# Dense expert values with tokens as output rows, an end that runs tile by tile, and a new split of the low parts between VectorE and GpSimd

## What is computed

```python
h = rmsnorm(x, g_mix)
q, k, v, f, B, C, xc, g_attn, g_conv = split(h @ w_in)
a = forgetting_attention(q, k, v, log_sigmoid(f + b_f))      # 8 heads x 64
c = B * causal_depthwise_conv3(C * xc)
x = x + (sigmoid(g_attn) * (a @ W_up_attn) + sigmoid(g_conv) * (c @ W_up_conv)) @ w_out
h = rmsnorm(x, g_ffn)                                        # expert retrieval ("PEER")
ids, gates = top 16 of 128 x 128 product keys, for each of 8 heads
x = x + sum over the 128 chosen of gates * gelu(h . u[id]) * v[id]
x = x + sigmoid(rmsnorm(x, g_ple) @ w_ple_gate) * (p @ w_ple_proj)
return rmsnorm(x, g_final)
```

## Time and profile before

| | |
|---|---|
| median of 3 runs | 1931.49 us (1930.06 to 1932.35) |
| the profiled execution | 1934.96 us |
| its span, first to last instruction | 1933.1 us |
| PE busy | 1854.1 us (96%) |
| DVE busy | 1271.2 us (66%) |
| POOL busy | 1137.2 us (59%) |
| ACT busy | 750.4 us (39%) |
| mean granted clock of TensorE | 0.983 |

### The profile page before, as it was taken

How to read it: one execution, slowest core, us unless ns; L and a number is a source line. 1 busy time by engine, 2 the same in 40 slices (tenths; PEclk the granted TensorE clock), 3 DMA queues, 4 the chain that set the end, 5 groups by cost and what they waited for, 6 DMA issues and landing times.

```text
span 1933.1 us, 24399 instructions
## 1 busy us (share of the span) xinstructions
PE 1854.1 (96%) x9045; PEld 1611.0 (83%) x9045; DVE 1271.2 (66%) x2244; ACT 750.4 (39%) x1190; POOL 1137.2 (59%) x666
## 2 busy tenths in 40 slices
PE   6999999989999999999999999989999998989987
PEld 5777788878888888888888888889999998989976
DVE  6355422357899778888988960146688677768643
ACT  5433322333232344444444442433344443434331
POOL 6322344433354476776767764478888888877430
PEclk9999999989999999999999999999999999999998
DMA  5222122322344435454554546659999999999511
GB/s 196 78 66 66 58 99 95 120 67 87 103 140 145 147 131 215 172 180 174 186 192 173 185 172 235 216 166 323 331 328 343 325 347 326 327 335 349 194 33 44
DMA packets 187509, 360.90 MB, mean 187 GB/s; under 512 B 17408, under 2 KB 123904, under 8 KB 185728
## 3 DMA queue, kind: packets, MB, share of 16 engines
q1 hardware_dynamic: 143328, 231.77, 36.5%
q0 software_dynamic: 22528, 67.19, 9.4%
q10 hardware_dynamic: 21536, 60.40, 8.4%
HBM read 298.44 MB, written 60.82 MB: 186 GB/s over the span
## 4 chain that ended last, share of the span: by engine, by line
PE 75%; POOL 17%; issue 3%; DMA 2%; DVE 1%; ACT 1%; ACTq 0%; SPq 0%; DVEq 0%
PE bank L745 36%; PE bank L553 11%; PE bank L555 10%; PE bank L554 10%; POOL wl L492 7%; POOL picked L520 6%; PE bank L770 2%; POOL gout L527 2%; POOL rows_h L527 2%; POOL rows_ex L527 1%; DMA raw<-stream 1%; PE bank L649 1%; PE bank L669 1%; PE bank L723 1%; PE bank L639 0%
## 5 line engine op out<-in xcount | busy, mean ns | idle before, releaser
L492 POOL TENSOR_TENSOR wl<-raw,wh 128x1024 fp32r<-128x1024 f32 x298 | 737.9, 2478 | 670.3 <-ACT wh L847 668.7
L847 ACT ACTIVATE wh<-raw 128x1024 fp32r<-128x1024 f32 x338 | 356.5, 1055 | 383.7 <-PE bank L555 195.2
L553 PE MATMUL bank<-hh,wh 128*128 128x512 f32 (+1 forms) x1056 | 396.6, 376 | 30.5 <-DVE x L1400 19.2
L745 PE MATMUL bank<-hh,wh 128*128 128x512 f32 x1024 | 400.3, 391 | 0.8 <-ACT scores L1002 0.8
L745 PE MATMUL bank<-hh,wl 128*128 128x512 f32 x1024 | 400.9, 391 | 0.0
L745 PE MATMUL bank<-hl,wh 128*128 128x512 f32 x1024 | 399.6, 390 | 0.0
L555 PE MATMUL bank<-hh,wl 128*128 128x512 f32 (+1 forms) x1056 | 389.4, 369 | 0.0
L554 PE MATMUL bank<-hl,wh 128*128 128x512 f32 (+1 forms) x1056 | 389.3, 369 | 0.0
L553 PEld LDWEIGHTS bank<-hh,wh 128*128 128x128 f32 x1056 | 202.6, 192 | 60.7 <-DVE x L1400 21.5
L745 PEld LDWEIGHTS bank<-hh,wl 128*128 128x128 f32 x1024 | 192.2, 188 | 37.8
L745 PEld LDWEIGHTS bank<-hl,wh 128*128 128x128 f32 x1024 | 192.3, 188 | 36.9
(11 more groups left out here) (211 smaller groups left out, 2503.6 us busy)
## 6 DMA issues: line engine op xcount, KB each, us to landing
raw<-stream SPq DMA_DIRECT2D x338, 512.0 KB
score_dram<-gout ACTq DMA_DIRECT2D x128, 256.0 KB, 2.5
gate_dram<-stage ACTq DMA_DIRECT2D x12, 2048.0 KB, 7.5
gate<-gate_dram SPq DMA_DIRECT2D x16, 1536.0 KB
score_in<-score_dram SPq DMA_DIRECT2D x128, 192.0 KB
x<-xT SPq DMA_DIRECT2D x4, 512.0 KB, 5.5
picked<-score_dram,score_at POOLq DMA_INDIRECT x128
outT<-outb SPq DMA_DIRECT2D x8, 256.0 KB, 2.2
```

Source lines behind the costliest of these rows:

```text
L492: nc.gpsimd.tensor_tensor(wl[:, n % SL, :], raw[:, n % RAW, :], wh[:, n % SL, :].bitcast(F32), ALU.subtract).then_inc(lo_done, 1)
L553: nc.tensor.matmul(out, ah, bh, start=start, stop=False)
L745: last = nc.tensor.matmul(psum[u % 2][:], w(weights, U_DENSE + u, c), tokens[c][:, :], start=c == 0 and which == 0, stop=c == DC - 1 and w ...
L847: nc.scalar.activation(wh[:, n % SL, :], raw[:, n % RAW, :], ACT.Copy).then_inc(hi_done, 1)
```

## The change

The V units keep the layout in which they lie in DRAM: one unit is one block of 128 experts by 1024 features, loaded in pieces of 4 KB. The activations become the stationary operand and the values the moving one: per block 3 token tiles x 2 halves x 3 = 18 matmuls of 512 columns, summed over all 128 blocks in three pairs of PSUM banks. `x` itself is transposed into these banks first, by float32 matmuls with the identity (`turn_x`, 8 for each tile), so `add_values` goes. `act_h` and `act_l` are one ring of 8 blocks, and the GELU uses two banks instead of three. The sum over the fetched rows is kept in SBUF (`sparse_sum`), starts from `x` of tile 0, and has 8 row slots and a lag of 5 steps instead of 6 and 4. DVE makes the low part of every second V unit. The end has tokens as rows and runs tile by tile in the order 1, 2, 0, 3: the squares are summed inside ACT's instruction, the norm is applied by a matmul with a scaled identity which also transposes (`turn_scaled`), and the last four blocks are computed tile by tile.

```diff
-HB = 4
+LAST = 4
+RING = 8
-ROWS = 6
-ROW_LAG = 4
+ROWS = 8
+ROW_LAG = 5
+END_ORDER = (1, 2, 0, 3)
 def low_by_dve(n):
-    return U_V0 + SL <= n < U_PLE and n % 3 == 0
+    return U_V0 + SL <= n < U_PLE and n % 2 == 0
...
+def turn_x(tile, pair):
+    for c in range(DC):
+        last = nc.tensor.matmul(pairs[pair][:, c * P:(c + 1) * P], x[:, c, tile * P:(tile + 1) * P], ident[:],
+                                start=c % 4 == 0, stop=tile == 0 and c % 4 == 3)
+    return last
...
+                if u == NK - TAIL_U + 1:
+                    pe.wait_ge(quad_out, QUADS)
+                    turn_x(0, 2).then_inc(x_turned, 1)
+                    turn_x(1, 1)
+                elif u == NK - TAIL_U + 5:
+                    pe.wait_ge(sum_copied, 1)
+                    turn_x(2, 2)
+def block_values(b, tile):
+    at = slice((tile - 1) * P, tile * P)
+    for half in range(2):
+        cols = slice(half * T, (half + 1) * T)
+        last = three(pairs[tile][:, cols], act_h[:, b % RING, at], act_l[:, b % RING, at],
+                     wh[:, (U_V0 + b) % SL, cols], wl[:, (U_V0 + b) % SL, cols], False, b == NK - 1)
+    return last
+for b in range(NK - LAST):
+    wait_low(pe, U_V0 + b)
+    pe.wait_ge(wsplit, b + 1)
+    for tile in range(1, TT):
+        if b == 0 and tile == TT - 1:
+            pe.wait_ge(wsplit, RING)
+            turn_x(tile, tile)
+        last = block_values(b, tile)
+    last.then_inc(unit_used, 1)
+def turn_scaled(tile, pair):
+    for c in range(DC):
+        last = nc.tensor.matmul(pairs[pair][:, c * P:(c + 1) * P], xt[tile][:, c * P:(c + 1) * P], scaled[:, tile, :],
+                                start=True, stop=True)
+    return last
+for tile in range(1, TT):
+    for b in range(NK - LAST, NK):
+        ...
+        last = block_values(b, tile)
+    if tile > 1:
+        pe.wait_ge(x_copied, tile - 1)
+        turn2(tile - 2)
+pe.wait_ge(row_added, HK)
+turn2(2)
...
 def add_row(k):
     dve.wait_ge(rows_in[k % ROWS], 16 * (k // ROWS + 1))
-    nc.vector.scalar_tensor_tensor(out=picked_sum[:], in0=vrow[k % ROWS], scalar=weight, in1=picked_sum[:],
-                                   op0=ALU.mult, op1=ALU.add).then_inc(row_added, 1)
+    nc.vector.scalar_tensor_tensor(out=sparse_sum[:], in0=rows[:, k % ROWS, :], scalar=pick_w[:, k:k + 1],
+                                   in1=sparse_sum[:], op0=ALU.mult, op1=ALU.add).then_inc(row_added, 1)
...
+def std_of(tile):
+    nc.scalar.activation(squares[:], xt[tile], ACT.Square, accum_out=ssq2[:, tile:tile + 1]).then_inc(squared2, 1)
+    act.wait_ge(squared2, tile + 1)
+    nc.scalar.activation(std2[:, tile:tile + 1], ssq2[:, tile:tile + 1], ACT.Sqrt, bias=eps[:],
+                         scale=1.0 / D).then_inc(std2_ready, 1)
+std_of(0)
+for n in range(U_PLE - SL, U_PLE - LAST):
+    next_high(n)
+std_of(1)
+std_of(2)
+high2(0)
+std_of(3)
+for n in range(U_PLE - LAST, U_PLE):
+    next_high(n)
+high2(1)
+high2(2)
+embeddings(0)
+high2(3)
+embeddings(1)
...
+for half in range(2):
+    for i in range(TT):
+        ple_gate(half, i)
+        if half == 1 and i == 2:
+            turn3(0)
+            turn3(1)
+turn3(2)
+turn3(3)
```

More of the change, by code:

```diff
@@ L65 @@
 TAIL_U = 18
-GELU_BANKS = 3
-OUT_BANKS = 3
+LAST = 4
+RING = 8
 TILE_ORDER = (1, 2, 3, 0)
@@ L165, in peer_block_kernel @@
         x = sb("x", [P, DC, T], F32)
[L166 to L174, removed]
+        tokens = ExitStack()
+        hh = sb("hh", [P, DC, T], F32R, tokens)
+        hl = sb("hl", [P, DC, T], F32R, tokens)
+        tokens.close()
+        rows = sb("rows", [P, ROWS, D], F32)
         raw = sb("raw", [P, RAW, UW], F32)
@@ new lines, in _, with weights, embedding @@
+            pe.wait_ge(row_added, HK)
+            turn2(2)
+            def weights(part, n, parts, k, order):
+                return part[:, n % SL, :].rearrange(order, j=4, k=parts)[:, k]
+            def embedding(half, tile):
+                i = TT * half + tile
+                if i >= 2:
+                    pe.wait_ge(emb_out, i - 1)
+                bank = psum[4 + i % 2].rearrange("p (j w) -> p j w", j=4)
+                for k in range(2):
+                    at = slice(k * T + tile * P, k * T + (tile + 1) * P)
+                    n = U_PLE + 1 + half
+                    last = three(bank, wh[:, U_PLE % SL, at], wl[:, U_PLE % SL, at],
+                                 weights(wh, n, 2, k, "p (j k w) -> p k j w"), weights(wl, n, 2, k, "p (j k w) -> p k j w"),
+                                 k == 0, k == 1)
+                last.then_inc(emb_ready, 1)
@@ new lines, in _, with ple_gate @@
+            pe.wait_ge(x_copied, 2)
+            for half in range(2):
+                wait_low(pe, U_PLE + 1 + half)
+                for tile in range(TT):
+                    embedding(half, tile)
+                if half == 0:
+                    pe.wait_ge(x_copied, 3)
+                    turn2(3)
+            def ple_gate(half, i):
+                tile, step = END_ORDER[i], TT * half + i
+                cols = slice(tile * P, (tile + 1) * P)
+                if half == 0:
+                    pe.wait_ge(hl2_ready, 2 * (i + 1))
+                if step >= 2:
+                    pe.wait_ge(sg_ready, step - 1)
+                bank = psum[6 + step % 2].rearrange("p (j w) -> p j w", j=4)
+                for c in range(DC):
+                    n = U_GATE + 4 * half + c // 2
+                    if i == 0 and c % 2 == 0:
+                        wait_low(pe, n)
+                    last = three(bank, hh[:, c, cols], hl[:, c, cols],
+                                 weights(wh, n, 2, c % 2, "p (j k w) -> p k j w"), weights(wl, n, 2, c % 2, "p (j k w) -> p k j w"),
+                                 c == 0, c == DC - 1)
+                last.then_inc(gate_ready, 1)
@@ L838, in _, with turn3 @@
+            def turn3(i):
+                pe.wait_ge(diag3_ready, i + 1)
+                if i >= 2:
+                    pe.wait_ge(out_ready, 2 * (i - 1))
+                turn_scaled(END_ORDER[i], i % 2).then_inc(turned3, 1)
+            for half in range(2):
+                for i in range(TT):
[5 more added lines that the diff above has]
+            turn3(3)
         @block.scalar
@@ new lines, in high2, with embeddings @@
+            def high2(i):
+                cols = slice(END_ORDER[i] * P, (END_ORDER[i] + 1) * P)
+                for half in range(2):
+                    act.wait_ge(hf2_ready, 2 * i + half + 1)
+                    nc.scalar.activation(hh[:, 4 * half:4 * (half + 1), cols],
+                                         hf2[:, half, :].rearrange("p (c t) -> p c t", c=4), ACT.Copy).then_inc(hh2_ready, 1)
+            def embeddings(half):
+                for tile in range(TT):
+                    i = TT * half + tile
+                    act.wait_ge(emb_ready, i + 1)
+                    nc.scalar.activation(emb[half][:, tile, :], psum[4 + i % 2], ACT.Copy).then_inc(emb_out, 1)
@@ new lines, in _ @@
+            std_of(0)
[12 more added lines that the diff above has]
+            embeddings(1)
+            act.wait_ge(emb_ready, 2 * TT)
+            for n in range(U_PLE, U_GATE):
+                high(n + SL)
@@ L1468, in weight_stream @@
+            scale3(3)
+            out(2)
+            out(3)
 def weight_stream(np, w_in, w_branch, w_out, w_peer_q, peer_u, peer_v, w_ple_gate, w_ple_proj):
```

390 lines of the change are left out of this document (216 added, 174 removed).

## The result

The changed kernel takes 1946.8 us (median of 4 runs, 1943.25 to 1950.04) against 1931.92 us (4 runs, 1930.06 to 1932.78) for the kernel before beside it: a ratio of 1.0078, 95% interval 1.0056 to 1.0100, so slower by 0.8%. The profiled execution of it took 1950.04 us, its span is 1948.3 us, the mean granted clock 0.987.

A forecast was written before the change was run, and what follows sets the result against it. POOL was taken to set the pace of V-stage steps 0 to 97. At 5.0 us a step the stage ends at 1867, plus 80: 1947 against a span of 1933.1, so 1931.5 + 14 = 1946 us; range 1880 to 1985.

The forecast's parts named there:

- the exclusion: V stage: a DVE instruction reading two SBUF tensors and a POOL instruction exclude each other, 0.55 us of POOL's time each.
- PE can run up to 8 blocks ahead of POOL's `low`: V stage: this cover was to make the smaller activation ring and two GELU banks cost nothing.
- The pairs: V stage: a DVE low and adjacent row add block POOL about 2.3 us, costing about 1.6, or 2.0 behind POOL's low.
- The start: Start of the V stage: turn_x's float32 matmuls make everything behind 6 us later; step 0's low moves to about 1289.
- The 98 steps: V stage, POOL's steps: 98 of 5.0 us are 490, less 7 us in the first steps, ending at 1772.
- The rest: V stage after POOL's steps: 22 PE blocks, 90 us, 2 for a turn, 3 for DMA; stage ends at 1867.
- The end: After the V stage: 80 us, 3 less than before, including about 6 us of embedding matmuls waiting for their two banks.
- Row adds that cost little: Rival, V stage: row adds cost POOL little or nothing; 4.3 us a step, kernel at 1878, scale of 1876; 15%.
- DMA term: V stage, in the rival of cheap row adds: 1.51 MB a step at 352 GB/s needs 4.28 us.
- A price below 0.5 us: Rival, V stage: adds fall into one phase of POOL's sequence, 0.25 to 0.5 us each; 1887 to 1926 us; 20%.
- The break-even of 0.54 us: V stage: price for each DVE instruction, 4.86 us for a step, at which the change neither gains nor loses.
- Full exclusion: Rival, V stage: POOL also holds DVE through each whole fetch; 5.35 us a step, 1980 us; 12% with other slower causes.

The follow-up runs named there:

- e1: Changed kernel with each row add replaced by a reduction of the same row (one SBUF input), weighted sum left out: 1896.7 us, ratio 0.9824.
- e2: Kernel before, its row add reading the fetched row twice (two SBUF inputs) instead of the sum in PSUM: 1970.03 us, ratio 1.0193.
- e4: Changed kernel with DVE making the low part of every V unit from the ninth on: 1900.77 us, ratio 0.9829.
- e6: Changed kernel with ACT copying the first half's embeddings ahead of the second and third tiles' high parts: 1940.27 us, ratio 1.0041.
- e10: Changed kernel with all V low parts from the ninth on DVE, both embedding copies early, and LOW_LAG 1 instead of 2: 1869.54 us, ratio 0.9681.
- e11: Changed kernel with LOW_LAG = 1 instead of 2 alone (DVE's low parts one step earlier): 1925.49 us, ratio 0.9978.
- e9: Changed kernel with all V low parts from the ninth on DVE and both embedding copies ahead of the last tile's high part: 1896.34 us, ratio 0.9829.
- e8: Kernel before with DVE making the low part of every V unit from the ninth on: 1950.14 us, ratio 1.0084.
- e12: Kernel before with DVE making every second V low part, and LOW_LAG = 1: 1909.07 us, ratio 0.9889.

## Why the prediction was right

**The mechanism is shown.** POOL sets the pace before and after, and the row adds take part in the exclusion as soon as both of their inputs lie in SBUF. One input less removes the loss (e1), one more creates it in the kernel before (e2), and with POOL's own work taken away the kernel gains 46 us although fetches are still held up (e4). The signs were: idle time only as "issue" (yes), 4.9 to 5.1 us for a step (4.88, at the lower edge), a mean of 1.2 to 1.4 us for the indirect transfers (263.0 / 196 = 1.34), row adds of over 3 us (10 of 98), and PE waiting for `wl` (38.7 us, none for `act_l`). PE's share was to be 82% and is 91% (380.7 of 420 us): a block keeps PE busy for 4.43 us, not 4.08. 0.13 us of this are the granted clock of 0.97, and the rest, such as the pipeline's tail ahead of each wait, was not taken apart. That PE can run up to 8 blocks ahead of POOL's `low` has it the wrong way round: PE waits for the `wl` of every block, as its rows show, and it is POOL that can be ahead.

**The mechanism was right; that the time came out within 1 us is partly luck.** Several terms were off, both ways.

*The pairs.* The step that two adjacent DVE instructions block a fetch for about 2.3 us failed. That was read from a POOL `low`; a fetch waits only for the first, in all 28 cases of the stretch. The hold-ups are 0.57 x 1.64 = 0.93 us for a step, as for instructions that lie apart (0.90), not 1.03. The working of the pairs had a slip as well: two steps hold 2.28 row adds, so 1.28 stand beside the pair, not one. With them it is (1.7 + 0.70) / 2 = 1.20 us and a step of 5.17 instead of 5.10; the 5.0 taken lies between 4.87 and either.

*The start.* The 16 early score fetches end at 1286.4 us, against 1282.7 before: 3.7 us later, not 6. POOL's first `low` of the V stage does stand at 1288.9 us, as if the sum's 1289 were right, but step 0's `low` is DVE's now, and this is step 1's.

*The 98 steps.* They end at 1767.1 us instead of 1772. From 1286.4 that is 480.7 us, where the sum had 483 (490 less 7): 4.90 us for a step with the first ones in it. Steps 0 to 2, 9.7 us together, are lighter, as reckoned; steps 3 to 97 take 4.96 us each.

*The rest.* From there to the end of the V stage at 1864.0 it is 97 us, not the 95 reckoned (90, a turn, and DMA). So the stage ends 3 us earlier than the sum's 1867. The end takes 84.3 instead of 80 us, since PE waits 7.9 us instead of 6 for ACT's copies and runs at 1.2 GHz behind the wait. e6 shows that this wait is on the path: with 7.1 us of it gone at one place and 4.7 back at another, the end is 2.9 us shorter. Together -3 and +4.3 us are the difference between the span of 1948.3 and the sum's 1947. The profiled execution is 3.2 us above the median of its kernel, that of before was 3.0 us above its own, so the two drop out.

**The rivals.** *Row adds that cost little* did not happen, but their time was 1876 and e1 gave 1896.7: the step was right, 4.29 us against 4.3. In its profiled execution, the shortest at 1888.66 us, the V stage ends at 1802.7 us instead of 1798 and 84 us follow instead of 80; its median lies 8 us above that execution. Its DMA term, 4.28 us as a floor at 352 GB/s, is refuted for the new layout by e10 at 4.07 us. *A price below 0.5 us* is not the changed kernel's (0.57), but it exists: 0.41 in e2, 0.44 in e11, where the total falls to 1925.5. The break-even of 0.54 us lies within what a shift of one step does to the price (0.57 to 0.44), and between the prices of two executions of the same V stage (0.57 and 0.52). So the sign of this result hung on the phase, as that rival said, and the forecast had no means to tell: that part of it is luck. *Full exclusion* is refuted: the row add of 1501.18 starts inside the fetch of 1500.34 and takes 1.27 us, and the step is 4.88, not 5.35. In e10, where POOL makes no `low` in the stretch, 136 two-input instructions start inside a fetch, and none takes more than 1.29 us.

On two SBUF inputs the trace agrees with "Who interferes with whom" in "SBUF — State Buffer" of the Trainium skill: DVE's `low` and POOL's `low`, which both read SBUF, wait for each other (DVE's took 3.44 us at 1506.39, and POOL's waited at 698.70), and e1 and e2 show the same loss for indirect transfers. It differs in two points, and the measurement decides. The section infers that a DVE `tensor_tensor` does not hold up the descriptor work of a transfer on GpSimd; here the 32 fetches that start inside DVE's `low` take 1.63 us at the mean instead of 0.95. And an indirect transfer does not hold the ports for its whole instruction, as the 136 instructions of e10 show.

**What stays open.** The rows show what a price is made of, the part of a DVE instruction that is left when a fetch starts; but which offset gives which price was not mapped, and e11 is the only run that moved nothing else. e10 shows that DVE's earlier `low` is worth 27 us over e9; that this goes through the slots freed for SP is what the waits say, but PE also gets that `wl` sooner, and the two were not separated. e8 was not run with `LOW_LAG = 1`, so what the layout is worth then isn't known beyond the 40 us between e12 and e10, which differ in the split as well. Nor was it tried what e10 would give with the sum back in PSUM.

## What to carry to other kernels

Count the SBUF inputs of every DVE instruction that shares a stage with POOL: moving an accumulator from PSUM to SBUF left the row add at 1.27 us where nothing stood in its way, and cost the fetches that started inside it 0.6 us at the mean and up to 1.0. A layout can be right and yet lose, if the engine that it frees is not the one that sets the pace; here the spare DVE time was worth 46 us once it took all of POOL's low parts, and another 27 us when DVE made them, and so freed the load slots, one step sooner. A DMA share near 1.0 is no proof of a ceiling while the issuing queue waits for slots (e9 and e10).

## What the runs showed that was not expected

An indirect transfer on POOL gets by between two back-to-back DVE instructions (1.74 us at 1500.34, where waiting for both would have made it about 2.9; 28 of 28 such fetches), while a POOL `low` waited through both (3.09 us). One core's DMA moved 378 GB/s over 350 us, at a share of 1.03, where 352 GB/s at 0.98 (e1) had looked full. And shifting DVE's low part by one step, with the same work on every engine, moved the kernel by 21 us (e11).
